# q, k, v beside the LRU: raw q and k rows copied out of PSUM by ScalarE, and a new order of projections and gates in a period

## What is computed

```
def mixer(h, w_in, conv_w, conv_b, lru_wa, lru_ba, lru_wx, lru_bx, lru_lambda, q_norm_g, k_norm_g, ...):
    proj = h @ w_in
    q, k, v, x_lru, y_lru = jnp.split(proj, cuts, axis=-1)
    q = rms_norm(q.reshape(B, S, N_Q_HEADS, HEAD_DIM), q_norm_g, QK_EPS)
    k = rms_norm(k.reshape(B, S, N_KV_HEADS, HEAD_DIM), k_norm_g, QK_EPS)
    q = apply_axial_rope(q, cos_r, sin_r, cos_c, sin_c).astype(h.dtype)
    k = apply_axial_rope(k, cos_r, sin_r, cos_c, sin_c).astype(h.dtype)
    ...
    xc = centred_depthwise_conv(x_lru, conv_w, conv_b)
    h_fwd = rg_lru_scan(xc, lru_wa[0], lru_ba[0], lru_wx[0], lru_bx[0], lru_lambda[0], False)
    h_bwd = rg_lru_scan(xc, lru_wa[1], lru_ba[1], lru_wx[1], lru_bx[1], lru_lambda[1], True)
    lru = (h_fwd + h_bwd) * jax.nn.gelu(y_lru.astype(jnp.float32))

def rg_lru_scan(xc, wa, ba, wx, bx, lam, reverse):
    r = jax.nn.sigmoid(jnp.einsum('bshi,hij->bshj', xh, wa) + ba).reshape(B, S, D_LRU)
    i = jax.nn.sigmoid(jnp.einsum('bshi,hij->bshj', xh, wx) + bx).reshape(B, S, D_LRU)
    log_a = -LRU_C * r * jax.nn.softplus(-lam.astype(jnp.float32))
    a = jnp.exp(log_a)
    u = jnp.sqrt(-jnp.expm1(2.0 * log_a)) * (i * xf)
    ...
```

## Time and profile before

| | us |
|---|---|
| median of 3 runs | 1797.85 |
| lowest and highest | 1796.04, 1798.97 |
| the profiled execution | 1797.65 |
| its span | 1795.9 |
| PE, DVE, ACT, POOL busy over the span | 1537.2, 1101.6, 891.9, 508.2 |
| mean granted clock of PE | 0.926 |

### The profile page before, as it was taken

How to read it: one execution, slowest core, us unless ns; L and a number is a source line. 1 busy time by engine, 2 the same in 40 slices (tenths; PEclk the granted TensorE clock), 3 DMA queues, 4 the chain that set the end, 5 groups by cost and what they waited for, 6 DMA issues and landing times. The chain is left out here.

```text
span 1795.9 us, 29351 instructions
## 1 busy us (share of the span) xinstructions
PE 1537.2 (86%) x8922; PEld 1293.9 (72%) x8923; DVE 1101.6 (61%) x1968; ACT 891.9 (50%) x1447; POOL 508.2 (28%) x366
## 2 busy tenths in 40 slices
PE   5999958888847999999999999975699999999920
PEld 5999936666536888888888888863477778778810
DVE  7555049889877766766767677644654443545245
ACT  4233245756737555555555555522255544556323
POOL 1222023353440021111111112112255353455218
PEclk9999979999969999999999999986699999999955
DMA  8665344434323011111121111114478767786574
GB/s 293 252 235 214 121 142 141 151 120 152 129 101 124 30 53 65 64 53 53 65 72 53 53 53 53 43 58 163 141 235 264 226 173 209 205 267 153 114 244 165
DMA packets 119338, 247.02 MB, mean 138 GB/s; under 512 B 18146, under 2 KB 71394, under 8 KB 119268
## 3 DMA queue, kind: packets, MB, share of 16 engines
q1 hardware_dynamic: 89328, 158.54, 25.8%
q0 software_dynamic: 12528, 45.62, 10.8%
q10 hardware_dynamic: 17412, 41.96, 6.1%
HBM read 151.71 MB, written 94.37 MB: 137 GB/s over the span
## 5 line engine op out<-in xcount | busy, mean ns | idle before, releaser
L1380 DVE TENSOR_TENSOR d_probs_t_lo<-d_pt_ps,d_probs_t_hi 128x512 fp32r<-128x512 f32 x256 | 164.3, 683 | 118.6 <-ACT d_probs_t_hi L1322 118.1
L1322 ACT ACTIVATE d_probs_t_hi<-d_pt_ps 128x512 fp32r<-128x512 f32 x256 | 139.3, 596 | 150.8 <-PE d_pt_ps L1209 144.7
L1366 DVE TENSOR_REDUCE d_neg_max<-d_s_ps 128x1 f32<-128x1024 f32 x128 | 155.5, 1215 | 5.7 <-PE d_s_ps L1198 5.7
L108 PE MATMUL e_a_ps<-up_hi,e_xt_hi 128*128 x336 | 138.8, 413 | 14.4 <-issue 11.5
L108 PE MATMUL acc<-k_hi,wl_hi 128*128 128x256 f32 x512 | 147.6, 288 | 3.7 <-DVE k_lo L453 2.4
L1227 PE MATMUL d_ot_ps<-d_probs_t_hi,d_v_split 128*128 128x256 f32 x512 | 139.7, 307 | 12.7 <-DVE d_probs_t_lo L1380 10.4
L109 PE MATMUL acc<-k_lo,wl_hi 128*128 128x256 f32 x512 | 146.7, 287 | 0.0
L110 PE MATMUL acc<-k_hi,wl_lo 128*128 128x256 f32 x512 | 146.6, 286 | 0.0
L1305 ACT ACTIVATE d_probs<-d_s_ps,d_neg_max 128x1024 f32<-128x1024 f32 x128 | 143.3, 1119 | 5.0 <-DVE d_neg_max L1366 5.0
L1209 PE MATMUL d_pt_ps<-ident,d_probs 128*128 128x128 f32 x1024 | 133.9, 274 | 4.4 <-ACT d_probs L1305 3.3
L109 PE MATMUL e_a_ps<-up_lo,e_xt_hi 128*128 x336 | 134.7, 401 | 0.0
(11 more groups left out here) (325 smaller groups left out, 4168.7 us busy)
## 6 DMA issues: line engine op xcount, KB each, us to landing
up_raw<-in_exp_w SPq DMA_DIRECT2D x32, 1024.0 KB, 9.9
down_raw<-in_exp_w SPq DMA_DIRECT2D x16, 1024.0 KB, 14.9
h_dram<-d_h_tile SPq DMA_DIRECT2D x17, 512.0 KB, 2.7
sum_dram<-d_h_tile SPq DMA_DIRECT2D x17, 512.0 KB, 3.5
h_dram<-v_all ACTq DMA_DIRECT2D x16, 512.0 KB, 4.2
ht_hi_dram<-k_hi ACTq DMA_DIRECT2D x8, 1024.0 KB, 4.2
ht_lo_dram<-k_lo ACTq DMA_DIRECT2D x8, 1024.0 KB, 6.8
c_hi<-ht_hi_dram SPq DMA_DIRECT2D x16, 512.0 KB, 4.2
```

The costliest lines, as they stand in the source:

```text
L108: pe.matmul(out, lhs[0], rhs[0], start=first, stop=False)
L1322: act.activation(pt_hi[:, c * HALF:(c + 1) * HALF, h % 2], pt_ps[c][:], ACT.Copy).then_inc(pth_done[c], 1)
L1366: dve.tensor_reduce(nm[:, u, h:h + 1], s_ps[h % 2][:], AX, ALU.max, negate=True).then_inc(nm_done, 1)
L1380: dve.tensor_tensor(pt_lo[:, part, h % 2], pt_ps[c][:], pt_hi[:, part, h % 2].bitcast(F32), ALU.subtract)\
```

## The change

ACT gets one more instruction per tile: `xr[u]` is filled with the raw q and k rows out of `pj[u]`. It waits until the rotation (DVE's and GpSimd's part) of two tiles before has read `xr[u]`. `normed` multiplies `xr[u]` in place. PE's wait for `normed` is left out, since v's copy comes after the new copy on ACT.

The order changes on three engines. PE: both projections of a period first, then transposes and half the gates, twice. ACT: split, square, copies for both tiles, then the first tile's eviction, the first half's tanhs, the second tile's eviction, decays, the second half's tanhs, root, first tap. DVE: the second tile's rotation ahead of `gated_x` and `product`, both sums of squares together ahead of the scans.

```
@@ front (PE)
                 if t >= 2:
                     pe.wait_ge(v_done, t - 1)
-                    pe.wait_ge(xr_done, t - 1)
@@ PE, the periods
-                for m in range(2):
-                    if m < len(group):
-                        front(group[m])
-                    if m < len(turned):
-                        back(turned[m])
+                for t in group:
+                    front(t)
+                for half in range(2):
+                    if half < len(turned):
+                        back(turned[half])
                     if g < NU:
-                        gates(g, m)
+                        gates(g, half)
@@ square (ACT)
                 act.activation(sq[u], pj[u][:, 0:QKW], ACT.Square).then_inc(sq_done, 1)
+                if t >= 2:
+                    act.wait_ge(a_done, t - 1)
+                    act.wait_ge(b_done, t - 1)
+                act.activation(xr[u], pj[u][:, 0:QKW], ACT.Copy).then_inc(copied, 1)
@@ ACT, the periods
                 square(group[0])
+                if len(turned) > 1:
+                    split(turned[1])
+                if len(group) > 1:
+                    square(group[1])
                 if g:
                     evict(turned[0])
                 if g < NU:
                     gate_tanhs(g, 0)
-                    decays(g)
-                if len(turned) > 1:
-                    split(turned[1])
-                if g < NU:
-                    root(g)
-                if len(group) > 1:
-                    square(group[1])
                 if len(turned) > 1:
                     evict(turned[1])
                 if g < NU:
+                    decays(g)
                     gate_tanhs(g, 1)
+                    root(g)
@@ normed (DVE)
-                if t >= 2:
-                    dve.wait_ge(b_done, t - 1)
-                    dve.wait_ge(a_done, t - 1)
-                dve.wait_ge(v_done, t + 1)
-                dve.tensor_tensor(by_head(xr[u]), by_head(pj[u][:, 0:QKW]),
+                dve.wait_ge(copied, t + 1)
+                dve.tensor_tensor(by_head(xr[u]), by_head(xr[u]),
@@ DVE, the periods
+                if len(turned) > 1:
+                    rotate(turned[1])
                 if g:
                     gated_x(g - 1)
                     product(g - 1)
-                if len(turned) > 1:
-                    rotate(turned[1])
-                squares(group[0])
+                for t in group:
+                    squares(t)
                 if 0 < g < NU:
                     scans(g - 1)
                     output(g - 1)
-                if len(group) > 1:
-                    squares(group[1])
```

More of the change, by code:

```diff
@@ L591, in qkv_lru @@
         v_done = sem("v_done")
+        copied = sem("qk_copied")
         xr_done = sem("xr_done")
```

## The result

The changed kernel takes 1815.43 us (median of 4 runs, 1813.14 to 1819.65) against 1797.64 us for the kernel before: 1.0102 times as long, with a 95% interval of 1.0082 to 1.0122. Forecast were 1819 and "slower". Its profiled execution took 1815.67 us, with a span of 1813.9 and a mean granted clock of 0.924.

A forecast was written before the change was run, and what follows sets the result against it. It took the PE-ACT exchange, with exposed decays and a low clock, to bound the stage: periods of 37.1 us (15.2 + 3.53 + 17.3 + 1.06) against 33.0, the stage ending 21.7 us later, 1819 us, range 1811 to 1827.

The forecast's parts named there:

- (a) to (e): Steps from F through first eviction, table load, first half's tanhs, second eviction and decays, ending at F + 15.2 us.
- F: The moment at which the last matmul of a period's second projection ends on PE.
- (d): ACT's eviction of the second tile, again 2.22 us, ending at F + 10.5.
- (b): ACT from the start of the first eviction up to the first tanh: 2.22 us, to F + 3.62.
- (f): Second half's first tanh to the next period's first projection: 2.16 us at full clock, 3.53 when it is down.
- (g): PE's two projections back to back: 17.3 us at full clock; the first after a stop takes 1.06 more.
- rival 1: The clock holds through PE's stop at the decays, 34.7 us a period: 1802.5 us; chance 0.14.
- DVE is there in time: At the stage's end, the last root ends at 521.9, 6 us before DVE's last sum of squares.
- What DVE loses is mostly one wait: In the kernel before, DVE waits 18.4 us in 6 times for ACT's square of the second tile.
- rival 3: Projections first free DVE, periods fall to 30.4 us, decays lying beside PE's work: 1773 us; chance 0.05.
- Rival 2: The clock falls twice, already in the first half, 2.1 us more in each of seven exchanges: 1834 us; chance 0.16.
- the page's price: The Trainium skill's table load of 2.66 us with drain, against the row's 1.30: 1829 us; chance 0.01.

The follow-up runs named there:

- the filled stop: Changed kernel plus nine extra fp32 matmuls of 256 columns per unit, results unread, in PE's stop ahead of the third gate matmul: 1800.72 us, ratio 1.0008.
- the load early: Changed kernel plus a one-element Tanh behind each first tap, bringing the table while ACT is idle: 1806.39 us, ratio 1.0043.
- order alone: Changed kernel without ACT's copies; the multiply reads PSUM and PE waits for it again: 1809.96 us, ratio 1.0062.
- the fastest order: Changed kernel with decays behind the second half's tanhs and the next first tap ahead of them: 1778.98 us; without copies 1768.46, again 1771.86.
- copies alone: Kernel before, in its old order, plus ACT's q and k copies and without PE's wait for the multiply: 1803.89 us, ratio 1.0026.

## Why the prediction held, and where it was off

**(a) to (e), the path from F to the second half.** Against F = 348.05, forecast and measured: first eviction 1.40 and 1.38; table load 3.62 and 3.60; second eviction (d) begins at 8.27 and 8.24; decays 10.5 and 10.3, as that eviction takes 2.05 and not (b)'s 2.22; the second half's first tanh 15.2 and 15.0. The copy was sized right at 0.60 (348.69 to the v copy at 349.27), and the decays' place is worth 16.4 us, as their removal from it showed.

**(f) and (g), the low clock.** Tanh to projection 3.53, measured 3.51, so that F to the next projection takes 18.48 us in each of the five full periods (forecast 18.73). Two projections 18.4, measured 18.2 to 18.8 in four of the five (366.53 to 385.17 is one). The choice of the lower clock against rival 1 decided 16 of the 18 us, and the filled stop measured it: 2.4 us a period, and the forecast was 37.1 - 34.7 = 2.4. Rival 1's 1802.5 is nearly what that kernel takes, 1800.7. It kept the low clock in period 0 (its 278.4 is the forecast's); at full clock there too it would have been 2.4 us less. The choice itself rested on a stop of 10 us and on one stretch of ragged work, neither of which is a stop of 4.5, so that it came out is in part luck.

**What was too long: the clock's return.** The last projection ended at 523.63, forecast 527.5, 3.9 us too late. Most of it is term (g) behind three of the exchanges, where the clock came back earlier. PE behind the F of period 5 of the changed kernel, to be held against 363.74 and 366.53 above:

```profile
438.16 3.44 PE L719 MATMUL gp<-xc,gate_w 128*128 128x512 f32 x4 [4.47 <-ACT lru_i L791]
440.95 0.88 PE L108 MATMUL pj<-wq_hi,c_hi 128*128 128x512 f32 x1
```

The stop is the same and the gates start at the same distance from F, but the first matmul of the projection takes 0.88, not 1.42, and the pair 17.3 (440.95 to 458.28). In periods 0 and 1 it was so too (0.96 and 1.04 for that matmul, 17.4 and 17.5 for the pairs), against 18.4 forecast: 2.8 us in the three. The slow start's price was taken from one place, period 0 of the kernel before, and used for every period. The six full exchanges, 0.25 too long each, are another 1.5 us. Against these, the other pairs and the last projection took 0.7 us more than forecast, in both directions; the rest is rounding. Nothing in the rows of before told at which matmul the clock comes back, and nothing in these does.

**The stage's end and the total.** Forecast +21.7, measured +17.9; the last sum of squares starts at 524.47, forecast 528.2. "Nothing behind it changes" held for these two executions, to 0.1 us, and that was luck as well: in the second profile of the same changed kernel the part behind the stage took 5.8 us more. The total was 1819.4 for 1815.67. "DVE is there in time" was too generous. The 6 us that it allowed run from the root's end, but DVE's product, 5.6 us long (518.96 to 524.55), comes in between. It ended just as the last square did (524.37), and in the kernel with PE's stop filled it ended 4 us later than the square.

**DVE within the period.** The first tap was forecast to be ready 24.3 us behind F, and was at 24.6 (371.38 + 1.23 - 348.05). The 41.9 us of DVE's waits for it are 6.0 each, where at least 4 had been forecast. Of the signs that the prediction named, three missed narrowly: two of the five pairs of projections took over 18.5 us (18.64 and 18.82), one of the five full periods 35.8 and not 36 to 38, and the stage's end came 17.9 and not 20 to 24 us later. The busy sum rose by 0.4 us a period, within the bounds of -0.3 to +1. So 0 was harmless where DVE waits anyway. It wasn't the operand's true price: where DVE is the bound, it is 9 us in the stage.

**"What DVE loses is mostly one wait", and rival 3.** The row was read rightly, but the wait was not what held the old order up; the sum didn't rest on it. Taking that wait away left a longer one for the tap, and the time rose. And rival 3's remedy, the decays beside PE's work, wasn't enough by itself: it gave 1799, not 1773, until the first tap, too, stood ahead of the decays. Then it gave 1779, and without the copies 1768 to 1772, 1.7 to 1.8% under the kernel before.

**Rival 2 and the page's price** fell: the clock went down once a period, and the load is worth 1.3 us.

**How the 17.9 us divide.** The parts overlap and don't add up: taking away the low clock gives back 15.9, the decays' place with part of the low clock 16.4, the load's place 8.9, the copies 5.3. The last two shorten the path from F to the second half, and not the stop: PE's waits there are 36.5 us in all without the copies and 36.6 with the load early, against 36.5.

## To carry to other kernels

Before moving work between two engines that trade a pair of buffers, walk the path from the last free-running instruction and write down what stands ahead of each release: one block of 4.7 us there cost 16 us in the stage. A long wait in a table isn't the bound until something shows that no other wait takes its place; look for the ring of instructions that wait for each other, and take the first instruction of the next unit ahead of work that it doesn't need. Where an engine stands still for some microseconds in every period, ask what the clock does after it, and price an operand's memory by its neighbours, not by its own row.

## What the runs showed of the hardware

In every period of the changed kernel the granted clock fell to 0.50 of 2.4 GHz within a stop of PE that the profile puts at 4.2 to 5.5 us. It came back between the first matmul of the projection and some 3 us into it, though in periods 2 to 7 the work in front of it is the same. Filling the stop with work that nobody reads gave 15.9 us back. A shorter stop went with a fall too, though not always: with the decays behind the tanhs the stops after the F of periods 2 to 4 were 2.3 to 2.5 us long, and the clock fell to 0.50 some 1.3 us after each, while it stayed at 1.00 after a stop of 2.4 in period 5.

A multiply that reads SBUF in place of PSUM took the same 0.78 us and lengthened its neighbours on DVE and GpSimd, by half a microsecond each where it stands.

Not expected, and not explained: the part behind the stage, whose code is the same in all kernels, varied from one profiled execution to the next. From the next stage's start to the end of the profiled span it took 1266.9 us before and 1267.0 in the changed kernel and in "order alone", but 1256.1 with the decays behind, 1257.4 with the square ahead of the root, 1271.3 without copies in the fastest order, and 1272.1 with copies alone. It isn't a matter of the kernel alone, since the changed kernel's second profile has 1272.9 for the first one's 1267.0. A single profiled total therefore misled by up to 12 us (with the square ahead of the root 1792.4, its median is 1804.25), where the next stage's start repeated within 0.6. What makes the difference stays open.
